# Opening of a decoder step reordered, rotary swaps issued by SyncE, head sums as two rounded passes

## The reference

```python
def _rms_norm(x, g):
    y = x * lax.rsqrt(jnp.mean(x * x, axis=-1, keepdims=True) + EPS) * g
def _mem_kv(mem, g, w_kv, k_g):
    kv = _rms_norm(mem, g) @ w_kv
    return _rms_norm(keys of kv, k_g), values of kv
...
h = _rms_norm(x, p["norm_mix"][i])
z = h @ p["w_in_att"][j]                     # q, k, v of the window, qx of the memory
q = _rope(_rms_norm(q, p["q_norm_att"][j]), pos)
k = _rope(_rms_norm(k, p["k_norm_att"][j]), pos)
o_self = _swa_prompt(q, k, v, p["sinks"][j])
...
qx = _rms_norm(qx.reshape(n, t, N_X_HEADS, HEAD_DIM), p["q_norm_x"][i])
o_x = _cross_attend(qx, mem_k[i], mem_v[i])
x = x + concatenate([o_self, o_x]) @ p["w_out"][i]
```

## Time and profile before

| | us |
|---|---|
| median of 3 runs | 1163.68 |
| lowest and highest | 1163.21, 1164.44 |
| the profiled execution | 1165.16 |
| its span, first to last instruction | 1163.4 |
| TensorE busy in it | 1143.0 (98%) |
| VectorE, ScalarE, GpSimd busy | 781.8, 533.0, 130.4 |

### The profile page before, as it was taken

The page is one execution under the profiler, slowest core; times in us unless marked ns, Lnnn a source line. Parts: engine busy times, 40 slices in busy tenths (PEclk is TensorE's granted clock), DMA queues, the critical chain, the costliest instruction groups (busy, mean ns, idle before and its releaser), DMA issues.

```text
span 1163.4 us, 22291 instructions
## 1 busy us (share of the span) xinstructions
PE 1143.0 (98%) x9026; PEld 1103.2 (95%) x9026; DVE 781.8 (67%) x1215; ACT 533.0 (46%) x920; POOL 130.4 (11%) x143
## 2 busy tenths in 40 slices
PE   7999999999999999999999999999999999999998
PEld 7899646999999999999999999999999999999998
DVE  5857776798568468568657545689866856756853
ACT  6743886367137227326434222436713722732630
POOL 0018853000000000000240131200000000000000
PEclk8999999999999999999999999999999999999999
DMA  8553231213313222312522321221321331231241
GB/s 309 203 162 119 61 139 61 92 59 124 107 39 112 106 72 102 115 51 94 214 75 73 146 82 66 73 100 56 135 99 48 110 109 72 91 125 43 102 137 48
DMA packets 23866, 120.18 MB, mean 103 GB/s; under 512 B 2788, under 2 KB 7012, under 8 KB 10740
## 3 DMA queue, kind: packets, MB, share of 16 engines
q1 hardware_dynamic: 18612, 100.93, 24.8%
q0 software_dynamic: 1632, 10.54, 2.4%
q10 hardware_dynamic: 3552, 7.74, 2.0%
HBM read 111.29 MB, written 5.69 MB: 101 GB/s over the span
## 4 chain that ended last, share of the span: by engine, by line
PE 88%; DVE 3%; POOL 3%; ACT 2%; issue 2%; DMA 1%; ACTq 1%; SPq 0%; DVEq 0%; POOLq 0%
PE zps L507 48%; PE zps L801 25%; PE ops L801 4%; PE zps L789 4%; POOL sm L1955 2%; PE ops L699 1%; PE tps L671 1%; ACTq L1750 1%; PE zps L545 1%; PE zps L625 1%; ACT w_hi L1445 1%; DMA memx<-memT 1%; DMA tmp<-z 1%; ACT act_hi L1445 0%; DVE sm L1090 0%
## 5 line engine op out<-in xcount | busy, mean ns | idle before, releaser
L507 PE MATMUL zps<-act_hi,w_hi 128*128 128x272 f32 x1664 | 349.2, 291 | 0.0
L507 PE MATMUL zps<-act_hi,w_lo 128*128 128x272 f32 x1664 | 344.3, 288 | 0.0
L507 PE MATMUL zps<-act_lo,w_hi 128*128 128x272 f32 x1664 | 343.5, 288 | 0.0
L801 PE MATMUL zps<-xf,wf 128*128 128x272 f32 x2304 | 297.0, 288 | 0.0
L801 PEld LDWEIGHTS zps<-xf,wf 128*128 128x128 f32 x2304 | 292.2, 188 | 0.8
L507 PEld LDWEIGHTS zps<-act_hi,w_hi 128*128 128x128 f32 x1664 | 262.6, 189 | 4.4 <-issue 2.9
L507 PEld LDWEIGHTS zps<-act_lo,w_hi 128*128 128x128 f32 x1664 | 261.9, 189 | 0.0
L507 PEld LDWEIGHTS zps<-act_hi,w_lo 128*128 128x128 f32 x1664 | 260.1, 189 | 0.0
L1445 ACT ACTIVATE w_hi<-w_stage 128x2048 fp32r<-128x2048 f32 (+2 forms) x65 | 115.6, 1779 | 161.6 <-PE zps L507 122.8
L952 DVE TENSOR_TENSOR w_lo<-w_stage,w_hi 128x2048 fp32r<-128x2048 f32 x57 | 133.4, 2341 | 50.9 <-ACT w_hi L1445 50.6
L1445 ACT ACTIVATE wf<-w_sum 128x1024 fp32r<-128x1024 f32 x64 | 68.0, 1062 | 195.4 <-DVE w_sum L970 90.7
(11 more groups left out here) (193 smaller groups left out, 1279.9 us busy)
## 6 DMA issues: line engine op xcount, KB each, us to landing
w_stage<-wst SPq DMA_DIRECT2D x91, 1024.0 KB, 4.9
kx<-xkT POOLq DMA_DIRECT2D x4, 1024.0 KB, 8.5
vx<-xv POOLq DMA_DIRECT2D x4, 1024.0 KB, 7.4
x_res<-xT ACTq DMA_DIRECT2D x2, 1088.0 KB, 8.3
tmp<-z ACTq DMA_DIRECT2D x32, 68.0 KB, 2.1
yT<-x_res ACTq DMA_DIRECT2D x7, 272.0 KB, 2.0
memx<-memT SPq DMA_DIRECT2D x4, 256.0 KB, 5.2
w_stage<-wst SPq DMA_DIRECT2D x4, 256.0 KB, 5.4
```

What stands on the lines that cost most here:

```text
L507: mm = pe.matmul(zps[slot][:, h, 0:n], w_[:, d, k, w:w + 128], r_[:, k, c0 + h * n:c0 + (h + 1) * n], start=(j == 0 and i == 0), stop=(j = ...
L801: mm = pe.matmul(bank, wf_hl[pw][:, fw, a, :], x_form(l, px, fx, a)[:, 0, :], start=(begin and a == 0 and j == 0), stop=(a == KC // 2 - 1 ...
```

## The change

- **Opening.** The load of the second piece of weights comes in two halves, which ScalarE copies apart. `norm_hi` and `norm_lo` of the first blocks, the token squares and their sums move to other places in ScalarE's and VectorE's lists. `split_hi(2, 1)` and `split_lo(2, 1)` now stand ahead of the last memory keys' copies, sums and roots. ScalarE makes a rounded copy `head_r` of the matrix that sums heads. The token sum moves from behind panel 0 into panel 1, behind its second block of channels. The turning of the last two memory keys moves from behind panels 1 and 2 to behind panels 2 and 3.
- **Head sums of layer 0.** ScalarE makes a rounded copy `sq_hi` of each square, VectorE the rest `sq_lo`, and TensorE sums both with `head_r`: four rounded matmuls in place of two fp32 ones. Sums n = 1, 3, 5, 7 use the bank `ops` instead of `tps`. Head sum n stands behind panel n + 2; 6 and 7 both behind panel 8, 8 behind 9, 9 behind 10.
- **Swaps.** SyncE issues them, between its loads.
- **Rotation.** VectorE does the last one (r = 7), ahead of its take of panel 11; GpSimd does 0 to 6.
- **Attention.** The low parts of one more product are made ahead of the last two maxima instead of between them.

```diff
+        def sums_at(i):
+            return {8: (6, 7), 9: (8,), 10: (9,)}.get(i, (i - 2,) if 2 <= i < 8 else ())
+        def sums_bank(n):
+            return ops if n % 2 and n < N_QX[0] else tps
...
-            sp.dma_start(stage[:, 1], wst[1]).then_inc(w_in[1], 16)
+            for h in range(2):
+                c = slice(4 * h, 4 * h + 4)
+                sp.dma_start(stage[:, 1, c], wst[1, :, c]).then_inc(w_in[1] if h else ld["w3"], 16)
+            def swapped(r):
+                sp.wait_ge(n_out, r + 1)
+                if r >= 2:
+                    sp.wait_ge(r_out, r - 1)
+                for to in range(0, 128, 32):
+                    sp.dma_start(tmp[to:to + 32, 4 + r % 2, :], z0[to ^ 32:(to ^ 32) + 32, r, :]).then_inc(r_sw[r % 2], 16)
+            def weight(q, d):
+                sp.wait_ge(w_los[d], q)
+                sp.dma_start(stage[:, d], wst[2 * q + d]).then_inc(w_in[d], 16)
...
             sp.dma_start(o_vs.rearrange("b s d -> s b d"), vb[ST:128, :, :]).then_inc(win_out, 16)
-            weights(Q_ATT + 2, Q_OUT0 + 1)
+            swapped(0)
+            weight(Q_ATT + 2, 0)
+            swapped(1)
+            swapped(2)
+            weight(Q_ATT + 2, 1)
+            swapped(3)
...
             def headsum(n):
+                if n < N_QX[1]:
+                    pe.wait_ge(h_rdy, 1)
+                    pe.wait_ge(n_lo, n + 1)
+                    free, bank = (ofree, ops) if n % 2 and n < N_QX[0] else (tfree, tps)
+                    take(free)
+                    for h in range(2):
+                        c = slice(h * HALF, (h + 1) * HALF)
+                        pe.matmul(bank[:, h, 0:HALF], head_r[:, :], sq_hi[:, n % 2, c], start=True, stop=False)
+                        mm = pe.matmul(bank[:, h, 0:HALF], head_r[:, :], sq_lo[:, n % 2, c], start=False, stop=True)
+                    mm.then_inc(n_ms, 1)
+                    free[0] = (n_dev, n + 1)
+                    return
...
             for i in range(12):
-                panel(Q_ATT + i // 4, i % 4, *act_hl[0], ready=normed(0) if i == 0 else None)
-                if i == 0:
-                    colsum(2, NT)
-                if i in (1, 2):
-                    turn_keys(1 + i)
-                if 1 <= i <= 10:
-                    headsum(i - 1)
+                panel(Q_ATT + i // 4, i % 4, *act_hl[0], ready=normed(0) if i == 0 else None,
+                      between=(lambda k, mm: colsum(2, NT) if k == 1 else None) if i == 1 else None)
+                if i in (2, 3):
+                    turn_keys(i)
+                for n in sums_at(i):
+                    headsum(n)
...
+            def square_lo(n):
+                dve.wait_ge(n_hi, n + 1)
+                dve.tensor_tensor(sq_lo[:, n % 2, :], tmp[:, n % 2, :], sq_hi[:, n % 2, :].bitcast(f32), ALU.subtract).then_inc(n_lo, 1)
+            def rotate_last():
+                z, other = z0[:, 7, :], tmp[:, 5, :]
+                dve.wait_ge(r_sw[1], 64 * 4)
...
-                        if p == (0 if j - 4 >= J_LAST - 1 else 1) and 0 <= j - 4 < G_L1:
+                        if p == (0 if j - 4 >= J_LAST - 1 or j - 4 == J_SS + 1 else 1) and 0 <= j - 4 < G_L1:
...
+                if i == 11:
+                    rotate_last()
                 take_scaled(q, p, z0[:, i, :])
                 if 0 < i < 10:
                     split_next(q, p)
...
-                if 1 <= i <= 10:
-                    head_norm(i - 1)
+                if i < 10:
+                    square_lo(i)
+                for n in sums_at(i):
+                    head_norm(n)
...
                 act.activation(tmp[:, n % 2, :], norm_src(n), ACT.Square).then_inc(n_sq, 1)
+                if n < N_QX[1]:
+                    act.wait_ge(n_sq, n + 1)
+                    copy(sq_hi[:, n % 2, :], tmp[:, n % 2, :]).then_inc(n_hi, 1)
...
+            split_hi(2, 1)
             keys_out(0)
             keys_out(1)
             root_keys(2)
             root_keys(3)
-            split_hi(2, 1)
+            act.wait_ge(ld["con2"], 16)
+            copy(head_r[:, :], headones).then_inc(h_rdy, 1)
...
-                if 1 <= i <= 10:
-                    root_heads(i - 1)
-                if 2 <= i <= 9:
-                    swapped(i - 2)
+                for n in sums_at(i):
+                    root_heads(n)
```

More of the change, by code:

```diff
@@ L122, in build_kernel @@
     con, _ = place("con", [128, C_N])
+    head_r, _ = place("head_r", [128, 128], f32r)
     hgain_n, _ = place("hgain_n", [128, 4])
@@ L174, in build_kernel @@
         n_sq, n_ms, n_inv, n_inv2, n_dev, n_out = (sem("n_" + s) for s in ("sq", "ms", "inv", "inv2", "dev", "out"))
-        r_sw, r_out = [sem(f"r_sw{i}") for i in range(2)], sem("r_out")
+        h_rdy, n_hi, n_lo = sem("h_rdy"), sem("n_hi"), sem("n_lo")
+        r_sw, r_out, r_last = [sem(f"r_sw{i}") for i in range(2)], sem("r_out"), sem("r_last")
         v_t, v_out = sem("v_t"), sem("v_out")
@@ L474, in _ @@
             sp.dma_start(o_vs.rearrange("b s d -> s b d"), vb[ST:128, :, :]).then_inc(win_out, 16)
-            weights(Q_ATT + 2, Q_OUT0 + 1)
+            swapped(0)
[4 more added lines that the diff above has]
+            swapped(3)
+            swapped(4)
+            weight(Q_OUT0, 0)
+            swapped(5)
+            swapped(6)
+            swapped(7)
+            weight(Q_OUT0, 1)
             sp.wait_ge(r_out, 2)
@@ L1014, in head_norm @@
                 y0, y0_sq = tmp[:, 2, :], tmp[:, 3, :]
[L1015 removed]
+                dve.scalar_tensor_tensor(out=halves(y0_sq), in0=sums_bank(n)[:, :, 0:HALF], scalar=HD * EPS, in1=halves(y0_sq),
                                          op0=ALU.add, op1=ALU.mult).then_inc(n_dev, 1)
@@ L1025, in head_norm_out @@
                                          op0=ALU.mult, op1=ALU.mult).then_inc(n_out, 1)
+            def square_lo(n):
[4 more added lines that the diff above has]
+                dve.wait_ge(r_sw[1], 64 * 4)
+                dve.tensor_tensor(z, z, cs[:, 0, :], ALU.mult)
+                link(dve.tensor_tensor(other, other, cs[:, 1, :], ALU.mult))
+                dve.tensor_tensor(z, z, other, ALU.add).then_inc(r_last, 1)
             def key_sums(m):
@@ L1347, in _ @@
             split_lo(1, 1)
+            for k in range(1, 4):
+                norm_lo(0, k, 0)
             for m in range(2):
                 key_norm(m)
-            for k in range(4):
-                norm_lo(0, k, 0)
             split_lo(2, 0)
+            for k in (1, 2):
+                add_x0(k)
             for k in range(4, KC):
                 norm_lo(0, k, 0)
+            for k in range(3, KC):
+                add_x0(k)
+            split_lo(2, 1)
             for m in (2, 3):
                 key_sums(m)
-            for k in range(1, KC):
-                add_x0(k)
             for m in (2, 3):
                 key_norm(m)
-            split_lo(2, 1)
             dve.wait_ge(ld["con2"], 16)
@@ L1743, in _ @@
             act.dma_start(con[:, 0:C_IDENT], cst[:, 0:C_IDENT]).then_inc(ld["con"], 16)
-            def swapped(r):
-                act.wait_ge(n_out, r + 1)
-                if r >= 2:
-                    act.wait_ge(r_out, r - 1)
-                for to in range(0, 128, 32):
-                    act.dma_start(tmp[to:to + 32, 4 + r % 2, :], z0[to ^ 32:(to ^ 32) + 32, r, :]).then_inc(r_sw[r % 2], 16)
             def take_memory(l, p):
@@ L1800, in _ @@
                     act.activation(msq[:, k, :], memx[:, k, :], ACT.Square).then_inc(m_sq, 1)
+            act.wait_ge(ld["w3"], 16)
+            copy(w_hi[:, 1, 0:4], stage[:, 1, 0:4]).then_inc(w_his_half, 1)
             act.wait_ge(w_in[1], 16)
-            copy(w_hi[:, 1, 0:4], stage[:, 1, 0:4]).then_inc(w_his_half, 1)
             copy(w_hi[:, 1, 4:8], stage[:, 1, 4:8]).then_inc(w_his[1], 1)
@@ L1817, in _ @@
             square_key(0, 1)
+            act.wait_ge(ld["x"], 16)
+            norm_hi(0, 0, 0)
             split_hi(1, 1)
+            for k in range(1, 4):
+                norm_hi(0, k, 0)
             root_keys(0)
@@ L1822, in _ @@
             take_memory(0, 3)
-            act.wait_ge(ld["x"], 16)
-            for k in range(4):
-                norm_hi(0, k, 0)
             take_memory(1, 0)
@@ L1831, in _ @@
             take_memory(1, 2)
+            for k in range(3):
+                square_x0(k)
             act.wait_ge(ld["x1"], 16)
-            for k in (4, 5):
-                norm_hi(0, k, 0)
-            for k in (0, 1):
-                square_x0(k)
-            for k in (6, 7):
+            for k in range(4, KC):
                 norm_hi(0, k, 0)
             take_memory(1, 3)
-            for k in range(2, KC):
+            for k in range(3, KC):
                 square_x0(k)
+            split_hi(2, 1)
             keys_out(0)
@@ L1977, in _ @@
             pool.wait_ge(ld["rope"], 16)
-            for r in range(8):
-                if r == 7:
-                    pool.wait_ge(n_ms, N_QX[0] + 2)
-                    pool.memset(qs[:, :, :, :], 0.0)
```

(2 more changed lines are left out.)

23 lines of the change are left out of this document (16 added, 7 removed).

## The result

| | before | changed |
|---|---|---|
| median, us | 1163.68 | 1175.27 |
| lowest and highest | 1162.67, 1165.02 | 1174.8, 1176.85 |
| span of the profiled execution | 1163.4 | 1173.3 |

The change made the kernel slower: ratio 1.0094, 95% interval 1.0081 to 1.0107, some 11 us. The forecast was 1167.2 with a range up to 1171.0, so the direction was right and the size was not.

What follows compares the result with a forecast made beforehand. TensorE, busy 98% of the span, was taken as the bound. The terms +0.5 - 2.8 + 7.0 - 1.2 gave +3.5 us on the median of 1163.68: 1167.2, with an 8-in-10 range of 1160.2 to 1171.0.

Steps and rivals of the forecast that it cites:

- Term 1: Opening, up to panel 3's start: the token sum's wait goes, idle for the reciprocal comes; +0.5 us.
- Term 2: TensorE's own work from panel 3's start to panel 11's end, with cheaper rounded head sums: -2.8 us.
- Term 3: TensorE's waits from panel 3's start to panel 11's end: late weights (4,0), norms piling up, rotations slowing passes; +7.0 us.
- the charge for the rotations: Behind the split of weights (4,0): GpSimd's rotations slow VectorE's norms and splits, at most 5.8 us more.
- the pile-up: Norms queue behind the late split of weights (4,0), so TensorE waits 4.1 us ahead of head sum 9.
- rival C: Everything slowed, nothing regained in the attention, the long idle lowers the clock again: +9.1 us, 1172.8, chance 0.07.
- Term 4: Attention, behind panel 11: no wait for the queries' copy, one low-part wait fewer; -1.2 us.
- Rival A: Load of weights (4,0) lands by 91.0, so norms do not pile up: -3.4 us, 1160.3, chance 0.18.
- Rival B: Load in time, but two norms at panel 8 and rotations keep VectorE late: -1.5 us, 1162.2, chance 0.20.

Runs made afterwards that it cites:

- the first experiment: The changed kernel with SyncE issuing the store o_vs ahead of the stores o_mk and o_mv instead of behind them: 1172.09 us, ratio 1.0057 to the kernel before.

## Why the prediction was right in direction and wrong in size

- **Term 1, right.** Forecast: idle 3.9, panel 2 at 6.0 + 1.5, panel 3 0.5 later. Measured: idle 3.82, panel 2 7.6, a mean clock of 0.79. On the time axis of the profile panel 3 came 0.3 earlier, but panel 0 started at 38.1 instead of 38.8; such starts lay between 36.2 and 39.7 in these profiles. Counted from panel 0, panel 3 is 0.4 later.
- **Term 2, right.** The four passes follow each other by 0.125 us, the wait for the keys' bank was 0.66 (0.6).
- **Term 3, wrong in size: the step that failed.** The store's issue (73.17 for 74.0) and the split behind it (93.82 for 95.1) came within 1.3 us of the forecast, though the delay lay in the issue of swap 0 (13.40 us) and not in the landing of the load (6.5 us). The chain of passes behind the split was right as well: 22.6 us to the end of norm 8's first pass in the forecast, 22.2 in the run with rotations on 16 columns. The step that failed is the charge for the rotations: "Were all four norms and two splits so slowed, it would be 4 x 1.0 + 2 x 0.9 = 5.8 more", of which 2.9 was taken. Measured, the same stretch holds 9.2 us of slowing, 8.5 in the time from its first to its last pass. The norms' last passes and the splits make 5.1 of it, near the forecast's full 5.8; 4.1 is in the low parts of the squares and the norms' second passes, which are two-input passes as well and stood in the sum at their length alone. The sum that should have been made is VectorE's list for two panels beside the rotations, 16 us, against TensorE's 13.
- **Two errors partly offset.** TensorE's waits from panel 8 on were 8.9 us against 7.0, within the bounds 4.1 to 9.9. But without the slowing the pile-up was 2.1 us of waits and not 4.1, as the split's low part was done at 97.8 and not at 99.3. That moving the store saved 4.3 and 3.8 us comes near the 4.1 by luck: these savings hold a loss of clock too.
- **The clock, put at nothing here.** Term 1 charged it for an idle of 3.9 us; term 3 had 7 us of waits and no charge. It cost 4.2 us beside the waits, of which 2.6 reached the end. It stood only in rival C, at 1.5 and with a chance of 0.07, and even that rival's 1172.8 lay below the 1175.27 measured.
- **Term 4, right in sign.** 0.8 us instead of 1.2, within its bounds.
- **Rival A fell.** The first experiment made its condition true, the load near 84 us, and the time was 1172.1, not 1160.3. The rule of the Trainium skill on issuing engines (page "DMA: Bandwidth & Descriptors", section "Issuing engines are not separate DMA queues"), which would have made it likelier, calls the time to initiate a DMA usually small relative to the DMA itself. That isn't borne out here: four DMAs of 68 KB took 13.40 us to issue behind the store in SyncE's queue.
- **Rival B had the mechanism and not the price.** In it the load is in time, and the doubled norms and the rotations keep VectorE late, for 0.4 to 3.5 us. With the load in time, the first experiment shows waits of 6.7 us for norms, and 1172.1 instead of 1162.2; the low parts of the squares were left out here too.
- **The rule on the shared port was the better guide.** The Trainium skill (page "SBUF — State Buffer", section "Who interferes with whom") says that VectorE passes with two inputs in SBUF and GpSimd instructions that read SBUF exclude each other. I applied it to the norms' last passes and the splits and not to the pass that the change adds; the time of that pass, 0.72 alone and up to 1.88 beside a rotation, agrees with the rule.

What stays open is when a wait brings the clock down: behind 2.80 us it stayed at 1.00, behind 1.77 it fell.

## What to carry to other kernels

Before an engine gets a new pass in each round, add up its own list for a round, at the durations that it has beside its neighbours, and compare it with the bound engine's round; here TensorE's one wait of 0.7 us for VectorE was the sign that such a list was nearly full, whatever its share of the span. A slowdown that was hidden costs nothing until the slack over it is spent, so taking it away in the kernel before tells little about the kernel after. And a wait of TensorE can have a second price in the clock of the work behind it: waits of 1.77, 3.63 and 3.82 us had it here, that of 2.80 had not.

## What was not expected of the hardware

A store of 992 KB from 124 partitions kept the DMAs issued behind it on the same engine from being issued: the next four small ones took 13.40 us, and before the change the one load behind it 10.50. Issued at 51.52, 21 us ahead of the next DMA of SyncE's list, as in the run with the store first, it held back nothing: there swap 0's four DMAs took 2.58 us to issue.
